# Key and query products turned one by one between slab points on VectorE, and slabs rounded ahead of coefficients on ScalarE

## What is computed (the reference, cut)

```python
def peer_ffn(h, w_pq, subkeys, u, v):            # first block's end: 8 heads x 16 experts per token
    ...
        u_sel = jnp.take(u, ec, axis=0)          # 128 rows of u per token
        act = jax.nn.gelu(jnp.einsum('chkd,cd->chk', u_sel, hc), approximate=False) * gc
        v_sel = jnp.take(v, ec, axis=0)
        return jnp.einsum('chk,chkd->cd', act, v_sel)

def second_block(...):
    h = h + 0.5 * swiglu(rmsnorm(h, ffn1_norm[l]), ...)
    h = h + hybrid_mixer(rmsnorm(h, mix_norm[l]), ...)
    h = h + 0.5 * swiglu(rmsnorm(h, ffn2_norm[l]), ...)

def rope(x, pos):
    x1, x2 = xf[..., : d // 2], xf[..., d // 2:]
    return jnp.concatenate([x1 * cos - x2 * sin, x2 * cos + x1 * sin], axis=-1)
```

## Time and profile before

| | us |
|---|---|
| median of 3 runs | 3513.28 (3505.88 to 3515.78) |
| the profiled execution's own time | 3516.8 |
| its span, first to last instruction | 3515.0 |
| PE busy in it | 3161.5 (90%) |
| DVE busy | 2564.0 (73%) |
| ACT busy | 1522.4 (43%) |
| woven half, about | 1421 to 2620 of the span |

### The profile page before, as it was taken

The page is one execution under the profiler, slowest core; times in us unless marked ns, Lnnn a source line. Parts: engine busy times, 40 slices in busy tenths (PEclk is TensorE's granted clock), DMA queues, the critical chain, the costliest instruction groups (busy, mean ns, idle before and its releaser), DMA issues.

```text
span 3515.0 us, 50299 instructions
## 1 busy us (share of the span) xinstructions
PE 3161.5 (90%) x18818; PEld 2492.4 (71%) x18818; DVE 2564.0 (73%) x4577; ACT 1522.4 (43%) x3103; POOL 795.9 (23%) x577
## 2 busy tenths in 40 slices
PE   7999999888887776899899899888999999999898
PEld 6888788744441121688667776667899988988898
DVE  6999353877777877788777688778866567667665
ACT  3222343254443333454444455545455444434443
POOL 1001454044345645133222232122100000000000
PEclk9999999999999999899899999999999999999999
DMA  3323244499999999799888899789866734453465
GB/s 126 96 90 95 84 132 134 162 406 420 409 419 412 413 384 421 279 417 413 318 314 350 325 399 389 275 325 363 334 185 205 254 114 147 139 168 109 144 186 156
DMA packets 185564, 923.56 MB, mean 263 GB/s; under 512 B 21776, under 2 KB 27152, under 8 KB 119520
## 3 DMA queue, kind: packets, MB, share of 16 engines
q0 software_dynamic: 73728, 536.90, 37.7%
q1 hardware_dynamic: 99248, 358.66, 30.4%
q10 hardware_dynamic: 12352, 24.87, 2.2%
HBM read 910.98 MB, written 9.37 MB: 262 GB/s over the span
## 4 chain that ended last, share of the span: by engine, by line
PE 62%; DMA 15%; DVE 11%; issue 5%; ACT 4%; POOL 2%; ACTq 0%; DVEq 0%; POOLq 0%; SPq 0%
PE psum L735 50%; DMA buffer_float<-in_peer_uv,buffer_uint 12%; PE psum L1093 6%; DMA raw_slabs<-in_slabs 3%; DVE buffer_float L2654 2%; POOL buffer_float L3337 2%; DVE slabs_remainder L2342 2%; PE psum L1316 1%; ACT slabs_rounded L1479 1%; DVE buffer_float L2812 1%; PE psum L1301 1%; DVE buffer_float32r L2247 1%; PE psum L1313 1%; PE psum L1399 1%; PE psum L1363 0%
## 5 line engine op out<-in xcount | busy, mean ns | idle before, releaser
L735 PE MATMUL psum<-buffer_float32r,slabs_rounded 128*128 128x256 f32 (+2 forms) x9568 | 1947.4, 303 | 44.3 <-DVE buffer_float32r L2247 27.7
L735 PEld LDWEIGHTS psum<-buffer_float32r,slabs_rounded 128*128 128x128 f32 x9568 | 1540.9, 192 | 195.4 <-issue 112.1
L735 PE MATMUL psum<-buffer_float32r,slabs_remainder 128*128 128x256 f32 (+2 forms) x4784 | 1436.4, 300 | 0.0
L2342 DVE TENSOR_TENSOR slabs_remainder<-raw_slabs,slabs_rounded 128x1024 fp32r<-128x1024 f32 x601 | 732.6, 1222 | 355.9 <-ACT slabs_rounded L1479 345.9
L1479 ACT ACTIVATE slabs_rounded<-raw_slabs 128x1024 fp32r<-128x1024 f32 x662 | 695.4, 1054 | 574.9 <-PE psum L735 429.0
L735 PEld LDWEIGHTS psum<-buffer_float32r,slabs_remainder 128*128 128x128 f32 x4784 | 916.4, 192 | 28.8
L3337 POOL DMA_INDIRECT buffer_float<-in_peer_uv,buffer_uint x512 | 647.8, 1265 | 1266.4 <-PE psum L1093 745.0
L1093 PE MATMUL psum<-buffer_float,buffer_float 128*64 128x512 f32 x1728 | 611.9, 626 | 195.3 <-ACT buffer_float L1806 175.2
L2654 DVE CUSTOM_DVE_ANT_0 buffer_float<-buffer_float,buffer_float 128x1024 f32<-128x1024 f32 x512 | 624.1, 1222 | 217.5 <-DMA buffer_float<-in_peer_uv,buffer_uint 207.0
L1093 PEld LDWEIGHTS psum<-buffer_float,buffer_float 128*64 128x64 f32 x1728 | 158.8, 140 | 550.4 <-issue 525.3
L1794 ACT ACTIVATE buffer_float<-buffer_float 128x1 f32<-128x1 f32 x512 | 101.8, 199 | 498.3 <-DVE buffer_float L2654 482.5
(11 more groups left out here) (214 smaller groups left out, 2054.7 us busy)
## 6 DMA issues: line engine op xcount, KB each, us to landing
raw_slabs<-in_slabs SPq DMA_DIRECT2D x682, 512.0 KB
buffer_float<-in_peer_uv,buffer_uint POOLq DMA_INDIRECT x512
buffer_float<-kept ACTq DMA_DIRECT2D x4, 874.5 KB, 6.9
buffer_float<-rows ACTq DMA_DIRECT2D x12, 256.0 KB, 9.7
xT<-in_xT ACTq DMA_DIRECT2D x4, 512.0 KB, 5.3
buffer_float<-in_consts ACTq DMA_DIRECT2D x8, 256.0 KB
kept<-buffer_float ACTq DMA_DIRECT2D x4, 512.0 KB
buffer_float<-kept ACTq DMA_DIRECT2D x2, 875.0 KB, 7.0
```

What stands on the lines that cost most here:

```text
L735: m = pe.matmul(out, a, b, start=start and j == 0, stop=stop and j == 2)
L2342: dve.tensor_tensor(slab_l[:, r, :], raw[:, r, :], slab_h[:, j, :].bitcast(F32), ALU.subtract)\
```

## The change

Three edits, all in the second block.

1. ACT's `point`: in the woven half slab t+3 is rounded first, and the coefficients of picks come after it.
2. DVE, retention, first run only (`h.off`): the four key products are no longer made together after both key points. A new function `turn_one` makes the two products of a bank and frees it; it is called after each of the two points. The difference and the sum come after, as before, and so does the wait for `kept_ret`.
3. DVE, attention, both runs (`head_qk`): point, query, point, key in place of point, point, query, key.

```diff
@@ ScalarE, point()
                 t = place[0]
                 place[0] += 1
-                if t < BLOCK2:
-                    coefficients(woven_by(t - 1))
                 if BLOCK1 + t + 3 < SLABS:
                     split_ahead()
                 if t < BLOCK2:
+                    coefficients(woven_by(t - 1))
                     if t in TURN:
@@ VectorE, rope_pair()
-                    else:
-                        for e, b in enumerate(banks):
-                            step(dve.tensor_tensor(t[:, e], psum[:, b, 0:n], c, ALU.mult))
-                            step(dve.tensor_tensor(t[:, 2 + e], psum[:, b, 0:n], s, ALU.mult))
-                    sync()
-                    for b in banks:
-                        dve.sem_inc(bank_free[b], 1)
+                        sync()
+                        dve.sem_inc(bank_free[banks[0]], 1)
                     step(dve.tensor_tensor(dst[:, 0, 0:n], t[:, 0], t[:, 3], ALU.subtract))
                     step(dve.tensor_tensor(dst[:, 1, 0:n], t[:, 1], t[:, 2], ALU.add))
                     sync()
                     dve.sem_inc(ret_rope, 1)
+
+                def turn_one(e, b, n, off):
+
+                    t, c, s = r.rt[:, :, 0:n], r.cos_r[:, off:off + n], r.sin_r[:, off:off + n]
+                    step(dve.tensor_tensor(t[:, e], psum[:, b, 0:n], c, ALU.mult))
+                    step(dve.tensor_tensor(t[:, 2 + e], psum[:, b, 0:n], s, ALU.mult))
+                    sync()
+                    dve.sem_inc(bank_free[b], 1)
@@ VectorE, retention head
-                    for _ in range(2):
+                    for e in range(2):
                         for _ in range(0 if i else index_banks(h)[0]):
                             next(scoring)
                         point()
+                        if h.off:
+                            turn_one(e, full(ks[e]), h.T, 0)
                     if h.off and i:
                         dve.wait_ge(kept_ret, 48 * i)
-                    rope_pair(r.rk, [full(bn) for bn in ks], h.T, 0)
+                    rope_pair(r.rk, [] if h.off else [full(ks[0])], h.T, 0)
@@ VectorE, attention head_qk()
-                    points(2)
+                    point()
                     rope_halves(r.aq, full(q), r.at_t[:, 0, 0:HALF], HALF, h.off)
+                    point()
```

## The result

| | before | after |
|---|---|---|
| median of the runs shown beside each other, us | 3514.53 (3505.88 to 3520.86, 4 runs) | 3470.54 (3468.65 to 3473.08, 4 runs) |
| ratio | | 0.9873, 95% interval 0.9857 to 0.9888 |
| span of the profiled execution | 3515.0 | 3468.9 |
| PE busy / mean granted clock | 3161.5 / 0.966 | 3143.2 / 0.975 |

The kernel became 44 us faster.

The account below looks back on a forecast made before the run. PE, busy 90% of the span, was taken as the bound, so its waits count. Terms -19.1 - 4.6 - 7 - 1.4 + 2.1 + 2.5 = -27.5 us from 3513.3 gave 3486, range 3472 to 3503.

Parts of the forecast that it names:

- Edit 2, retention: Retention: bank B freed earlier ends PE's stalls ahead of four value slabs, 19.1 us, plus 4.6 us of clock.
- two thirds: Retention: share taken of the 7.0 us of slow clock behind the stalls, 4.6 us, since slowness can move elsewhere.
- The DMA floor: Retention's 91.5 MB need 220 us at 416 GB/s, so far off; at 358 GB/s 256 us, gain at most 23.
- Edit 1 in attention: First-run attention: rounding 2.2 us earlier shortens DVE's waits; 7 us won, bounds 0 and 16.4, clock not counted.
- Edit 1, what it costs: Woven half: coefficients come one rounding (1.04 us) later, lengthening PE's waits for diagonals; losses of 2.1 and 2.5 us.
- 2.1 and 2.5: Diagonal waits: 2 x 1.04 us at two large ones; 2.5 us, from 0 to 5.2, at the other five.
- Edit 3: Second-run attention: query fills DVE's wait for a rounding; PE's waits shrink 1.4 us, bounds 0 and about 4.
- The saved time in retention: Rival: retention's gain returns as another wait; if 14 of 23.7 us return, about 3500; chance 0.17.
- the first rival: Retention's saved time comes back as new waits, slabs and picks being late; about 3500 us, chance 0.17.
- The ring of picks: Rival: the picks' ring sets the pace and later coefficients lengthen it; +11 to +63 us, 3524 or more; chance 0.07.
- PE was freed: Against the rival that PE's retention stall has another cause, leaving only attention: -4 us, about 3509; chance 0.06.
- More is won: Rival: all DVE waits of attention and the whole clock are won, -41 us: 3472; chance 0.10.

Follow-up runs that it names:

- b2: Changed kernel without edit 1 (edits 2 and 3 alone, coefficients ahead of the rounding everywhere): 3491.47 us, ratio 0.9934 to the kernel before.
- b3: Changed kernel with edit 1 kept only in first-run attention (points 150 to 176): 3483.31 us, ratio 0.9906 to the kernel before.
- f2: Changed kernel with edit 1 only from point 150 on, coefficients first before that: 3477.19 us, ratio 0.9881 to the kernel before.
- b1: Changed kernel with bank B in retention freed only together with bank C: 3494.24 us, ratio 0.9943 to the kernel before.
- c3: Changed kernel with edit 3 undone in the last attention head of the second run: 3476.28 us, ratio 0.9899 to the kernel before.
- d3: Changed kernel, old order in the second run's last attention head, one key product made two times more there: 3472.76 us, one execution.
- c1: Changed kernel with DVE's group sums made ahead of the slab remainder where a group of 64 picks ends: 3473.18 us, ratio 0.9890 to before.
- b4: Changed kernel with point, query, key, point in attention, both runs: 3472.29 us, ratio 0.9876 to the kernel before.

## Why the prediction was right in direction and short in size

**Edit 2, retention: right in mechanism.** Predicted 19.1 of stalls and 4.6 of clock, 23.7. Measured are 21.2 with edit 2 alone (mean of four) and 26 with edit 1 beside it. In the best of the four, that of the run with edit 2 alone, it is 26.2: of 20.8 us of waits 1.8 are left, so 19.0 went, and 7.2 us of slow clock with them, not two thirds, but all of it. In the other three (b2, b3, f2) PE waits 2.2 to 3.4 us at the second turn, and its matmuls take 2 to 3 us longer than in the best one. That the freeing of bank B is the cause was shown by b1 (21 us lost). The rule of the Trainium skill ("TensorE: Matmul & The Clock Gate", on the clock gate) that activity releases the slow default clock would have given 7.0 here, and the trace agrees with it where no wait is left. The last head's wait in c3 and d3 shows that a wait does not bring the slow clock each time.

**The DMA floor.** Retention ran at 362 GB/s. The 358 GB/s in the Trainium skill ("DMA: Bandwidth & Descriptors", Specifications) would have allowed 23 us; retention won more, 26 to 28.

**Edit 1 in attention: the sum right, in part by luck.** 7 us predicted, 7.4 measured (156.4 and 149.0, means). The kernel before was seen in an execution that was good there, so the two main profiles show only 5. DVE's waits for a rounding fell from 16.4 us to 2.3. But the prediction had the 7 us as waits, "the clock not counted", and PE's waits fell by only 4 us in the mean (27.7 to 23.7); the other 3 are matmuls that ran faster (granted clock over this part 0.89 to 0.90 in before, b2 and the kernels with edit 2 or 3 alone, 0.91 to 0.93 in b3, edit 1 alone and the two executions of all edits).

**Edit 1, what it costs: the step that failed.** Predicted +4.6 us (2.1 and 2.5). The cost itself is there: PE's waits for diagonals grew by 7.1 us (12.8 to 19.9). The two large ones went from 4.58 and 4.32 us to 5.15 and 3.29, where 1.04 more had been forecast for each. But "elsewhere in feed-forward and in 2002 to 2108 the edit moves nothing: slabs are rounded when they land" is wrong. I had followed who waits for a coefficient, and not who waits for the rounding behind it: DVE's remainder, and behind that the sums at a group's end and the merged tile. The trace of before had a row for it that I passed over, PE's waits for the sums, 1421 to 2620:

```profile
PE psum L1106 <- DVE buffer_float L2828: 9.1, 2, 6.4
```

They are 6.39 us at the first turn and 2.75 at the third, in attention; after the change 2.96 at the first are left. I even named both places, ACT coming out of the last retention head's root and out of the merged tiles, and counted them as a cost alone; 2.78 us of DVE are won at the first and 1.62 at the second. Measured, edit 1 wins 8 to 12 us outside attention (10.1 by the parts), so this term is off by 12 us or more, including its sign. With 10.1 won in place of 4.6 lost the sum would have been 42.2, not 27.5. That this is within 2 us of the result is partly luck: edit 2 was taken 2.5 us too high and edit 3 3.7 too low.

**Edit 3: right in mechanism, mis-sized.** Predicted 1.4 us of waits in the second run; 1.5 were measured (4.7 to 3.2), but with them 4 us of slow clock went in that execution. The median gain alone is 4.8 (0.4 to 9). I had left the clock out of this term, and out of attention's ("the clock not counted").

**The sum.** 21.2 for edit 2, 7.4 for edit 1 in attention, 10.1 for edit 1 elsewhere (4.8 of it in retention), 5.1 for edit 3: 43.8, against 40 to 44 measured.

**Rivals.** The saved time in retention did not come back with all three edits; without edit 1 some of it did (4.8 us in the mean, at the second turn), so the first rival was right about edit 2 and had not seen that edit 1 keeps it away. The ring of picks did not pace the kernel (its first feed-forward part, from the fourth slab to the down part, took 158.9 us before and 159.0 after), and PE was freed. "More is won" (3472) came closest, but for reasons that it did not hold: it doubled attention, and not what lay outside.

## What to carry to other kernels

When two steps change places on an engine, follow both queues: who waits for the step that comes later, and who waits for the one that comes earlier, with all that is queued behind that waiter. Good places here were those where the engine came out of a long wait of its own (ACT behind the root and behind the merged tiles), since what it then did first was already being waited for. And a buffer held by a consumer's grouping (four products, two banks, one release) can cost more than the consumer's work: here 21 us for a semaphore raised some microseconds late.

## What the runs showed of the hardware

- A stretch at half clock is not set by the length of the wait ahead of it alone: 2.68 and 3.59 us left the granted clock at 1.00, 2.69 us brought it to 0.50 in other kernels, at the same place of the program (one execution each).
- Retention's loads ran at 362 GB/s at a DMA share of 0.94 with PE busy 251.91 of 252.00 us, so that traffic, which I had thought might come to the fore, cost PE nothing.
- Taking a wait away from PE twice brought others of its size or more (5.64 us for 2.96 at the first turn in c1; 6.3 us more for ACT's copies and 3.8 more for diagonals in place of 8.7 us for keys in b4), with no change of the time.
